# Retention norm: the reciprocal root moved from GpSimd to VectorE, and two weight subtractions placed behind the scaling

## What is computed

```python
def layer_norm(x, g, b):
    mu = jnp.mean(xf, axis=-1, keepdims=True)
    var = jnp.mean(jnp.square(xf - mu), axis=-1, keepdims=True)
    y = (xf - mu) * lax.rsqrt(var + EPS)
    return (y * g + b)
...
ry = retention_chunkwise(rq, rk, rv)              # (B, S, 8, 64)
ry = layer_norm(ry, ret_norm_g, ret_norm_b).reshape(B, S, 512)
y_ret = jax.nn.silu(r_g) * ry
...
mix = jnp.concatenate([y_ret, y_dsa], axis=-1) @ w_out
x = x + rms_norm(mix, post_mix_g)
```

## Time and profile before

| | us |
|---|---|
| median of 3 executions | 1512.46 (1511.58 to 1512.67) |
| the profiled execution's own time | 1512.23 |
| its span in the profile | 1510.5 |
| PE busy | 1455.7 (96%) |
| DVE busy | 1080.6 (72%) |
| ACT busy | 621.9 (41%) |
| POOL busy | 307.9 (20%) |
| mean granted TensorE clock | 0.995 |

### The profile page before, as it was taken

How to read it: one execution, slowest core, us unless ns; L and a number is a source line. 1 busy time by engine, 2 the same in 40 slices (tenths; PEclk the granted TensorE clock), 3 DMA queues, 4 the chain that set the end, 5 groups by cost and what they waited for, 6 DMA issues and landing times.

```text
span 1510.5 us, 19666 instructions
## 1 busy us (share of the span) xinstructions
PE 1455.7 (96%) x7133; PEld 1175.6 (78%) x7133; DVE 1080.6 (72%) x1562; ACT 621.9 (41%) x1210; POOL 307.9 (20%) x375
## 2 busy tenths in 40 slices
PE   7999999999799899999899999999999999999997
PEld 7887888887686567777677888888887888888886
DVE  4749988999888778884487777777776666556543
ACT  5444443218525556556352222222222455443211
POOL 3544466503610354332200000000000000000000
PEclk9999999999999999999999999999999999999999
DMA  6322233317033111111224444444447876663111
GB/s 203 78 54 78 79 94 110 104 54 260 21 125 119 43 50 63 43 43 45 74 64 137 165 165 165 165 164 164 164 166 246 327 241 227 229 221 107 56 56 42
DMA packets 138111, 189.29 MB, mean 125 GB/s; under 512 B 13856, under 2 KB 76704, under 8 KB 138016
## 3 DMA queue, kind: packets, MB, share of 16 engines
q1 hardware_dynamic: 122528, 153.44, 31.4%
q10 hardware_dynamic: 15488, 34.61, 5.9%
HBM read 130.34 MB, written 57.67 MB: 124 GB/s over the span
## 4 chain that ended last, share of the span: by engine, by line
PE 79%; DVE 7%; issue 4%; DVEq 3%; ACT 3%; POOL 2%; DMA 1%; SPq 0%; ACTq 0%; POOLq 0%
PE ps L693 20%; PE ps L695 20%; PE ps L694 20%; PE ps L966 4%; PE ps L901 3%; PE ps L892 2%; DVEq L1832 2%; DVE sc L1816 2%; PE ps L884 2%; PE ps L883 1%; DVEq L1830 1%; PE ps L865 1%; DVE m L1829 1%; PE ps L821 1%; PE ps L701 1%
## 5 line engine op out<-in xcount | busy, mean ns | idle before, releaser
L1829 DVE MAX8 m<-sc 128x8 f32<-128x640 f32 (+5 forms) x176 | 162.2, 922 | 10.4 <-issue 2.0
L2376 POOL TENSOR_TENSOR smf<-smf,sml 128x1 f32<-128x1 f32 x16 | 9.1, 579 | 741.7 <-DVE smf L2283 627.3
L1831 DVE MATCH_REPLACE8 sc<-m,sc 128x640 f32<-128x640 f32 (+5 forms) x176 | 159.6, 907 | 0.8 <-issue 0.6
L693 PE MATMUL ps<-bh,ah 128*128 128x512 f32 x308 | 120.3, 390 | 0.0
L694 PE MATMUL ps<-bl,ah 128*128 128x512 f32 x308 | 119.9, 389 | 0.0
L695 PE MATMUL ps<-bh,al 128*128 128x512 f32 x308 | 119.9, 389 | 0.0
L693 PE MATMUL ps<-wbh,xth 128*128 128x512 f32 (+1 forms) x320 | 119.0, 372 | 0.0
L694 PE MATMUL ps<-wbl,xth 128*128 128x512 f32 (+1 forms) x320 | 118.1, 369 | 0.0
L695 PE MATMUL ps<-wbh,xtl 128*128 128x512 f32 (+1 forms) x320 | 118.0, 369 | 0.0
L2227 DVE TENSOR_TENSOR al<-ra,ah 128x512 fp32r<-128x512 f32 x77 | 53.2, 690 | 77.2 <-ACT ah L1581 77.0
L693 PE MATMUL ps<-th,ssh 128*128 128x512 f32 x240 | 93.6, 390 | 1.8 <-DVE u2b L2111 1.1
(11 more groups left out here) (307 smaller groups left out, 3751.8 us busy)
## 6 DMA issues: line engine op xcount, KB each, us to landing
raw<-in_w_in SPq DMA_DIRECT2D x50, 256.0 KB, 3.1
wt<-in_w_ffn_down SPq DMA_DIRECT2D x44, 256.0 KB, 7.2
down_sums<-wt ACTq DMA_DIRECT2D x44, 256.0 KB, 5.2
ra<-hidden_sums SPq DMA_DIRECT2D x44, 256.0 KB, 2.9
rb<-down_sums SPq DMA_DIRECT2D x44, 256.0 KB, 3.8
raws<-in_w_ffn_gate SPq DMA_DIRECT2D x21, 512.0 KB, 4.0
raws<-in_w_ffn_up SPq DMA_DIRECT2D x21, 512.0 KB, 5.3
ret_rows<-stg SPq DMA_DIRECT2D x32, 320.0 KB, 3.6
```

Source lines behind the costliest of these rows:

```text
L693: pe.matmul(o, ah, wh, start=start, stop=False, skip_group_check=resumes)
L1829: v.max(M8[:, :], sc_b)
L1831: v.match_replace(sc_b, M8[:, :], sc_b, PICKED)
```

## The change

`ret_scale` loses its wait for POOL. A new function `ret_root` on DVE computes the root between centering and scaling: it reads the bits of `vn` as an integer, turns it into a float, forms 0x5F3759DF minus half of it and takes the result as the bits of a first guess, halves and negates `vn`, and makes three Newton steps of three instructions each. These are 12 instructions on 128 x 16, all linked, and `ret_center`'s last one is now linked too. The four powers of this norm leave POOL. The two `wol` subtractions of pairs 1 and 2 now stand behind the pair's scaling.

```diff
-            v.tensor_scalar(cols["vn"], cols["ssn"], 1.0 / HD, EPS, ALU.mult, ALU.add).then_inc(s["v_lnv"], 1)
+            link(v.tensor_scalar(cols["vn"], cols["ssn"], 1.0 / HD, EPS, ALU.mult, ALU.add))
+
+        def ret_root():
+
+            y, t, half = cols["rsn"], cols["ssn"], cols["vn"]
+            link(v.tensor_copy(y, half.bitcast(I32)))
+            link(v.tensor_scalar(y.bitcast(I32), y, -0.5, float(0x5F3759DF), ALU.mult, ALU.add))
+            link(v.tensor_scalar(half, half, -0.5, None, ALU.mult))
+            for _ in range(3):
+                link(v.tensor_tensor(t, y, y, ALU.mult))
+                link(v.tensor_tensor(t, t, half, ALU.mult))
+                link(v.scalar_tensor_tensor(y, t, 1.5, y, ALU.add, ALU.mult))
...
             if step == 0:
-                dve.wait_ge(s["p_lnr"], hp + 1)
...
+            ret_root()
+            for step in range(4):
+                ret_scale(hp, step)
             if 1 <= hp < NP - 1:
                 out_weights_lo(2 * hp - 2)
                 out_weights_lo(2 * hp - 1)
-            for step in range(4):
-                ret_scale(hp, step)
...
             causal_scores(n)
-            if r == 5 and hp >= 1:
-                pool.wait_ge(s["v_lnv"], hp)
-                rsqrt(cols["rsn"], cols["vn"]).then_inc(s["p_lnr"], 1)
...
             ret_lo(NP - 2, half)
-        pool.wait_ge(s["v_lnv"], NP)
-        rsqrt(cols["rsn"], cols["vn"]).then_inc(s["p_lnr"], 1)
```

More of the change, by code:

```diff
@@ L256, in build @@
         v_link p_link v_nrm p_nrs t_nt a_nt t_ix a_rl v_acc p_caus v_mask p_tri p_rot
-        t_rb a_rb t_sc a_st p_st t_ro a_o a_silu p_zero v_lnv p_lnr v_y t_yr a_yrt
+        t_rb a_rb t_sc a_st p_st t_ro a_o a_silu p_zero v_y t_yr a_yrt
         t_lg v_lm a_ex t_tp a_tp t_pv a_ots t_ms a_ms v_ms a_mss p_mr x1_made a_fss p_fr fn_made
```

## The result

| | us |
|---|---|
| before, median of 5 executions | 1512.67 (1511.58 to 1513.61) |
| with the change, median of 5 | 1519.33 (1519.05 to 1521.10) |
| ratio | 1.0045, 95% interval 1.0035 to 1.0056 |
| profiled execution, its own time (before: 1512.23) | 1520.71 |
| its span (before: 1510.5) | 1519.0 |

The change makes the kernel 6.7 us slower between the medians.

The account below looks back on a forecast made before the run. DVE's norms and PE's masks, transposes and projection were taken to meet at pair 3's `y`, both bounding the stage; 1.9 + 1.1 - 0.5 + 2.4 = +4.8 us on 1512.23 gives 1517.0, range 1511.7 to 1519.6.

Parts of the forecast that it names:

- Part 1: Last two masks: 3.83 us of POOL's power go; pair 3's outputs copied by 404 to 406; PE waits 0.8, covered.
- Part 2: DVE's norms: root and link cost 10.6 us for four pairs, 8.74 of waits return; last `y` +1.86 us.
- the mask rival: Roots of pairs 0 to 2: six small instructions each wait out a 0.41 us mask, 2.5 us more: 1519.5; chance 0.10.
- the second rival: Norm stretch: POOL and DVE get out of each other's way, pair 3's `y` at about 428.5: 1512.2; chance 0.15.
- The rival by which small instructions are nearly free: DVE's root: links cost as little as 0.08 us per instruction, root 1.0 us per pair: 1508.2; chance 0.07.
- Part 3: Weight subtractions behind scaling: DVE's sum unchanged, projection starts at 412.1 instead of 415.09, PE early by 3 us.
- Part 4: Pair 3's centering: pair 2's `yrl` halves now run beside it and cost DVE 1.1 us, between nothing and 2.
- Part 5: Pair 3's transposes and projection: PE idles 5.4 us, clock falls to 0.50 for 6.1 us, costing 2.4 us.
- The statement on what bounds the stage: Stage end at pair 3's `y`: DVE's and PE's chains end within half a us; a gain needs both to shorten.
- my fast rival: DVE's root: small linked instructions cost 0.08 us, PE and DVE meet at about 424.5: 1508.2; chance 0.07.

Follow-up runs that it names:

- the trace with both roots: Changed kernel with POOL's four powers back at their old places, written to a column that nobody reads: 1516.17 us (1.0030); the traced execution took 1514.38.
- the no-root kernel: Changed kernel with the call of `ret_root()` left out: 1511.65 us (0.9993).
- the filler run: Changed kernel with 60 instead of 10 filler transposes on PE ahead of pair 3's transposes: 1518.86 us (1.0042).
- Two roots on each engine: Changed kernel with the roots of pairs 0 and 3 back on POOL, those of pairs 1 and 2 on DVE: 1514.48 us (1.0017).

## Why the prediction was right, point by point

The direction was right, the size too small: +4.8 us forecast, +6.7 measured between the medians, inside the range (+8.5 between the profiled executions, the clock's later falls included). The median of 1519.33 lies near the range's upper end.

*Part 1 (POOL's powers).* As put: pair 3's outputs were copied by about 404.4, PE waited 0.83 us for pair 0's `y`, both without effect. That the freed time is of no use is borne out by the trace with both roots.

*Part 2 (the root's price).* The spacing of 0.21 was right: the undisturbed root of pair 3 took 2.51 us. Those of pairs 0 to 2 took 2.78, 2.80 and 3.93, in all 1.9 us more than 4 x 2.52. About 1.0 of that is the `yrl` half at 399.73. The other 1.0 are seven small instructions that started within a mask and were held to its end, by 0.09 to 0.21 each. So the mask rival had the mechanism and not the size: it took a full mask of 0.41 for each, 2.5 us; that its 1519.5 is the recorded number nearest to the median is luck, for what it lacked came from the clock. Against this, the other instructions of pairs 0 to 2 met POOL 2.8 us less than before, as the second rival had said of two of them: the 2.18 and 2.27 of the earlier trace rows have no successor in the scaling, though pair 1's `wol` took 3.63 instead of 2.56. `y` of pair 3 ended 3.09 us later from the first centering, against 1.9 + 1.1 forecast. The sum was right by luck: +1.9 here and +1.0 in part 4 were cancelled by -2.8. The rival by which small instructions are nearly free is out: undisturbed, the root's instructions are busy 0.17, the two-tensor ones too. The Trainium skill, page "VectorE: DVE Perf Modes", section "The TRN2 errata", has a table by which they would take 0.077 and a remark that measurements want more; the trace agrees with the remark.

*Part 3 (the moved subtractions).* As put. The projection began at 410.72, 3.6 us earlier from the first centering; 3 had been said. Undoing the move alone gave 1.0036 against 1.0045, with intervals that overlap; in its trace PE's gap was 4.06 instead of 6.08.

*Part 4 (pair 2's halves).* The mechanism was right, the size was off: two instructions were hit, not one, for 2.1 us instead of 1.1, which holding the halves back gave back in full.

*Part 5 (the clock).* The clock fell, as put, but this term was mis-sized. I took the 6.1 us of the earlier trace rows; it stayed low 8.4 us behind the restart, and the loss between pair 3's transposes and the key products is 3.2 instead of 2.4. And I had priced one gap: "I see nothing that gives the delay back" left out that the clock can fall again later. It did at 480 (1.5 us), by chance as far as the other traces tell. The statement on what bounds the stage was right for the change and became wrong for the no-root kernel, where POOL bounds it, and I hadn't worked out that case: my fast rival's 1508.2 had PE and DVE alone in it, and even without any root the time was 1511.65.

## What to carry over

Taking a wait away gains only what it exceeds the work put in its place by: here 8.7 us of waiting went for 12 us of small linked instructions, 0.21 us each where nothing disturbs them. Look at both engines that meet at the end of a stage; here, freeing the one that wasn't last lengthened an idle gap. A gap of TensorE just ahead of dense work can cost twice: 6.08 us idle, then 3.2 us by the clock. The best version gave DVE only the two roots that nothing covered, left POOL those that were covered, and moved a POOL job out of the way of DVE's two-input instructions.

## What the runs showed of the hardware that I had not expected

- The granted clock fell in or behind PE gaps of 2.35 and 3.43 us, and at 480 behind one of 1.55 us in three traces but not in the others with the same gap; in one trace a gap of 3.02 us left it at 1.00. Two gaps of 1.67 and 1.18 us ahead of the projection left it at 1.00 in the changed kernel and lowered it (0.73 from 410 to 412) in the filler run. The length of a single gap doesn't decide it in these traces.
- VectorE and GpSimd hinder each other in both directions. A GpSimd subtraction of 128 x 512 held a 128 x 16 VectorE instruction with one tensor input for up to 1.25 us instead of 0.17, and a two-input one of 128 x 1024 for 2.26 instead of 1.22; VectorE's large two-input instructions stretched GpSimd's masks from 0.41 to about 1.4 us each. VectorE's small instructions let GpSimd's masks through at 0.41 to 0.44, and with them gone POOL was late (the run without a root): the slow root helped to keep POOL on time. The Trainium skill, page "SBUF — State Buffer", section "Who interferes with whom", calls the ports that the two engines share an exclusive lock: while one of the two holds it, the other blocks. The traces agree for the halves (1.20, 1.25, 2.26 us) and for small instructions beside masks: all seven in the root that started within one took 0.26 to 0.38 and ended 0.01 to 0.04 us behind it. By the page, an instruction with one SBUF input, as those of 1.20 and 1.25 us are, contends only in a mode that uses both ports; whether they ran in one, no run here shows. The traces don't agree with the lock for GpSimd's power: in the run with both roots the small instructions beside it, from 400.61 to 402.91, took 0.17 or 0.18.
- Two roots on each engine gave times from 1512.69 to 1518.39 in executions of the same kernel. Its trace has the clock fall in the gap of 3.43 and near 1170, but is of an execution of 1513.55, in the faster group, so those two falls alone don't make the slower group; what does wasn't found.
